# Conv FFN up products: one 512-column matmul for both input parts, bank copies on ScalarE, add and scale on GpSimd

## The reference, cut to what matters

```python
def conv_ffn(h, w_up, conv_w, conv_b, w_down):
    S = h.shape[1]
    u = h @ w_up
    up = jnp.pad(u, ((0, 0), (CONV_WIDTH_2 - 1, 0), (0, 0)))
    uc = conv_b + sum(conv_w[j] * up[:, j:j + S] for j in range(CONV_WIDTH_2))
    gate, val = uc[..., :D_FF_2], uc[..., D_FF_2:]
    return (jax.nn.silu(gate) * val) @ w_down
```

## Time and profile before

| | us |
|---|---|
| median of 3 runs (lowest to highest) | 1089.23 (1089.05 to 1089.32) |
| span of the profiled execution, first to last instruction | 1086.7 |
| PE busy in it | 1078.6 |
| DVE busy in it | 773.8 |
| ACT busy in it | 641.4 |
| POOL busy in it | 21.5 |

### The profile page before, as it was taken

One profiled execution on the slowest core, in us unless ns is written; L12 is line 12 of the kernel. 1 busy time (PEld: TensorE's weight loads), 2 busy tenths in 40 slices (PEclk: granted clock), 3 DMA queues, 4 the chain that ended last, 5 costly groups with the idle time before them and its releaser, 6 DMA issues.

```text
span 1086.7 us, 19341 instructions
## 1 busy us (share of the span) xinstructions
PE 1078.6 (99%) x7124; PEld 944.0 (87%) x7124; DVE 773.8 (71%) x1390; ACT 641.4 (59%) x1105; POOL 21.5 (2%) x47
## 2 busy tenths in 40 slices
PE   9999999999999999999999999999999999999998
PEld 8967899999988887888888999999877789999997
DVE  5977765555567767666756977878876757787876
ACT  5577664444466567566566555555766756555553
POOL 0000000000000000000010000000001000000000
PEclk9999999999999999999999999999999999999999
DMA  9642566666646563365515566565553435656562
GB/s 318 192 132 81 172 195 193 190 182 187 193 118 213 157 210 101 115 191 180 174 60 155 176 194 193 158 209 186 164 193 110 143 117 175 202 167 211 171 196 97
DMA packets 117774, 183.90 MB, mean 169 GB/s; under 512 B 6864, under 2 KB 70736, under 8 KB 117584
## 3 DMA queue, kind: packets, MB, share of 16 engines
q1 hardware_dynamic: 117280, 182.77, 53.7%
q10 hardware_dynamic: 432, 0.29, 0.1%
HBM read 181.99 MB, written 1.05 MB: 168 GB/s over the span
## 4 chain that ended last, share of the span: by engine, by line
PE 90%; DVE 6%; ACT 3%; issue 1%; DMA 1%; SPq 0%; DVEq 0%; ACTq 0%
PE ps L722 11%; PE ps L724 10%; PE ps L723 10%; PE ps L750 9%; PE ps L752 9%; PE ps L751 9%; PE ps L811 5%; PE ps L812 5%; PE ps L813 5%; DVE w_lo L1901 3%; PE ps L913 2%; PE ps L890 1%; PE ps L943 1%; PE ps L986 1%; DVE hid L2421 1%; ACT w_hi L1299 1%
## 5 line engine op out<-in xcount | busy, mean ns | idle before, releaser
L1901 DVE TENSOR_TENSOR w_lo<-w_stage,w_hi 128x1024 fp32r<-128x1024 f32 x336 | 403.5, 1221 | 171.0 <-ACT w_hi L1299 170.0
L1299 ACT ACTIVATE w_hi<-w_stage 128x1024 fp32r<-128x1024 f32 x336 | 349.1, 1054 | 172.0 <-PE ps L724 75.6
L750 PE MATMUL ps<-aT_hi,w_hi 128*128 128x256 f32 x992 | 281.6, 284 | 0.6 <-issue 0.4
L752 PE MATMUL ps<-aT_hi,w_lo 128*128 128x256 f32 x992 | 280.8, 283 | 0.0
L751 PE MATMUL ps<-aT_lo,w_hi 128*128 128x256 f32 x992 | 280.8, 283 | 0.0
L722 PE MATMUL ps<-w_hi,aT_hi 128*128 128x512 f32 x480 | 192.9, 402 | 1.9 <-DVE aT_lo L1915 1.3
L750 PEld LDWEIGHTS ps<-aT_hi,w_hi 128*128 128x128 f32 x992 | 190.3, 192 | 2.3 <-DVE w_lo L1901 0.7
L751 PEld LDWEIGHTS ps<-aT_lo,w_hi 128*128 128x128 f32 x992 | 190.3, 192 | 1.0
L752 PEld LDWEIGHTS ps<-aT_hi,w_lo 128*128 128x128 f32 x992 | 190.3, 192 | 0.0
L724 PE MATMUL ps<-w_hi,aT_lo 128*128 128x512 f32 x480 | 187.5, 391 | 0.0
L723 PE MATMUL ps<-w_lo,aT_hi 128*128 128x512 f32 x480 | 187.1, 390 | 0.0
(11 more groups left out here) (252 smaller groups left out, 1108.0 us busy)
## 6 DMA issues: line engine op xcount, KB each, us to landing
w_stage<-in_ffn_w_up SPq DMA_DIRECT2D x88, 512.0 KB, 4.7
w_stage<-in_a_w_qkv SPq DMA_DIRECT2D x72, 512.0 KB, 4.1
w_stage<-in_ffn_w_down SPq DMA_DIRECT2D x44, 512.0 KB, 3.5
w_stage<-in_w_up SPq DMA_DIRECT2D x32, 512.0 KB, 3.9
w_stage<-in_w_down SPq DMA_DIRECT2D x32, 512.0 KB, 4.3
w_stage<-in_b_w_qkv SPq DMA_DIRECT2D x24, 512.0 KB, 4.1
w_stage<-in_w_in SPq DMA_DIRECT2D x23, 512.0 KB, 5.1
w_stage<-in_w_out SPq DMA_DIRECT2D x8, 512.0 KB, 3.5
```

What stands on the lines that cost most here:

```text
L750: pe.matmul(o, wh, aT_hi[:, k, :], start=(k == 0), stop=False)
L752: last = pe.matmul(o, wl, aT_hi[:, k, :], start=False, stop=(k == KT - 1))
L1299: act.activation(w_hi[:, slot, :], w_in[:, slot, :], ACT.Copy).then_inc(hi_done[slot], 1)
L1901: dve.tensor_tensor(w_lo[:, slot, :], w_in[:, slot, :], w_hi[:, slot, :].bitcast(F32), ALU.subtract).then_inc(lo_done[slot], 1)
```

## The change

In the FFN's head and loop (ten of the eleven groups of each layer) the first two matmuls of a triple become one: `aT_hi` and `aT_lo` now lie side by side in one tensor `aT`, and the high weights meet both in one matmul with 512 moving columns. It writes a whole bank: the left half gets hi x hi (and later lo x hi), the right half hi x lo. The two halves are added afterwards: ACT copies the whole bank to SBUF (`both`, in the space of `xn`) and frees it, POOL adds the halves in place and then multiplies with `rbc` into `scaled`. DVE's `scale_up` goes away in these groups. ACT's `taps` wait for POOL (`scaled`). POOL waits for ACT's copy and for the taps of the group before, which read the same `scaled`; ACT's copy waits until POOL has read the same part of `both` for the group before. The weight splits move somewhat among these steps. The tail group keeps its three matmuls and DVE's `scale_up`.

```diff
-        aT_hi = sb("aT_hi", [P, KT, S], F32R)
-        aT_lo = sb("aT_lo", [P, KT, S], F32R)
+        aT = sb("aT", [P, KT, 2, S], F32R)
+        aT_hi, aT_lo = aT[:, :, 0, :], aT[:, :, 1, :]
...
+        both = xn[:].rearrange("p t (f s) -> p (t f) s", s=2 * S)
...
-                            pe.matmul(o, wh, aT_hi[:, k, :], start=(k == 0), stop=False)
-                            pe.matmul(o, wh, aT_lo[:, k, :], start=False, stop=False)
+                            if fold:
+                                pe.matmul(ps[:, bank(stg, names[f]), :], wh, aT[:, k, :, :].rearrange("p a s -> p (a s)"),
+                                          start=(k == 0), stop=False)
+                            else:
+                                pe.matmul(o, wh, aT_hi[:, k, :], start=(k == 0), stop=False)
+                                pe.matmul(o, wh, aT_lo[:, k, :], start=False, stop=False)
                             last = pe.matmul(o, wl, aT_hi[:, k, :], start=False, stop=(k == KT - 1))
...
-                dense_cols(S_, 0, 4, B4)
+                dense_cols(S_, 0, 4, B4, fold=True)
...
+            def second_half(stg, i, names, f):
+
+                act.wait_ge(*is_full(stg, names[f], i))
+                act.activation(both[:, f, :], ps[:, 4 + f, :], ACT.Copy).then_inc(drained[4 + f], 1)
...
+                def halves(stg, i, names, n, fs):
 
                     for f in fs:
-                        act.wait_ge(*is_drained(stg, names[f], i))
+                        if stg is not st["ffn_a_head"] or n > 1:
+                            act.wait_ge(s["scaled"], at(stg, "scaled", 4 * (n - 2) + f + 1, i))
+                        second_half(stg, i, names, f)
+
+                def taps(stg, i, names, j, n, fs):
+
+                    for f in fs:
+                        if n is None:
+                            act.wait_ge(*is_drained(stg, names[f], i))
+                        else:
+                            act.wait_ge(s["scaled"], at(stg, "scaled", 4 * (n - 1) + f + 1, i))
...
                 def convolve(stg, i, n0, names, j, n):
 
                     split(stg, n0, i)
-                    taps(stg, i, names, j, (0, 1))
+                    halves(stg, i, names, n, (0, 1))
                     split(stg, n0 + 1, i)
+                    taps(stg, i, names, j, n, (0, 1))
                     split(stg, n0 + 2, i)
                     gate(stg, i, n)
-                    taps(stg, i, names, j, (2, 3))
+                    halves(stg, i, names, n, (2, 3))
                     split(stg, n0 + 3, i)
+                    taps(stg, i, names, j, n, (2, 3))
...
+            def scale_up(stg, i, names, n):
+
+                for f in range(4):
+                    pool.wait_ge(*is_drained(stg, names[f], i))
+                    pool.tensor_tensor(both[:, f, 0:S], both[:, f, 0:S], both[:, f, S:2 * S], ALU.add)\
+                        .then_inc(s["half"], 1)
+                    pool.wait_ge(s["conv"], at(stg, "conv", 4 * (n - 2) + f + 1, i))
+                    pool.wait_ge(s["half"], at(stg, "half", 4 * (n - 1) + f + 1, i))
+                    pool.tensor_tensor(scaled[:, f, :], both[:, f, 0:S], rbc[:], ALU.mult).then_inc(s["scaled"], 1)
+
+            def scale_ffn(tag):
+
+                S_ = st[f"ffn_{tag}_head"]
+                pool.wait_ge(*is_drained(st[f"norm_ffn_{tag}"], "scale"))
+                scale_up(S_, 0, A4, 1)
+                scale_up(S_, 0, B4, 2)
+                S_ = st[f"ffn_{tag}_loop"]
+                with trips(pool, S_) as i:
+                    scale_up(S_, i, A4, 1)
+                    scale_up(S_, i, B4, 2)
...
                 def convolve(stg, i, n0, names, j, n):
 
                     split(stg, n0, i)
-                    scale_up(stg, i, names, (0, 1))
                     split(stg, n0 + 1, i)
                     taps(stg, i, j, n, (0, 1))
                     split(stg, n0 + 2, i)
-                    scale_up(stg, i, names, (2, 3))
+                    split(stg, n0 + 3, i)
                     taps(stg, i, j, n, (2, 3))
                     product(stg, i, n)
-                    split(stg, n0 + 3, i)
```

More of the change, by code:

```diff
@@ L287, in ffn @@
         up = {"cv": 4, "conv": 4, "silu": 1, "u": 1, "uhi": 1, "ulo": 1, "dve_step": 4}
+        folded = {**up, "half": 4, "scaled": 4}
         return [
@@ L448, in blocks_kernel @@
             "orstd", "osq", "hms", "dm", "ovar", "sig", "sq", "ms8", "rs8", "silu", "u", "uhi", "ulo", "msq", "pms", "prstd", "x_new",
-            "lam", "zeroed", "const_ready", "gate_w", "unit", "rd", "rdb", "bc", "ohi", "olo")}
+            "half", "scaled", "r2", "lam", "zeroed", "const_ready", "gate_w", "unit", "rd", "rdb", "bc", "ohi", "olo")}
         def is_full(stg, name, i=0):
@@ L732, in dense_rows, with dense_cols @@
                         after[q]()
-            def dense_cols(stg, i, n0, names, turned=None, after=None, order=BY_PAIRS, each=None):
+            def dense_cols(stg, i, n0, names, turned=None, after=None, order=BY_PAIRS, each=None, fold=False):
                 for q, (pair, deep) in enumerate(order):
@@ L1236, in ffn @@
                 with trips(pe, S_) as i:
-                    dense_cols(S_, i, 0, A4)
+                    dense_cols(S_, i, 0, A4, fold=True)
                     await_hidden(S_, 0, i)
                     down(S_, i, 4, range(2))
-                    dense_cols(S_, i, 6, B4)
+                    dense_cols(S_, i, 6, B4, fold=True)
                     await_hidden(S_, 1, i)
@@ L1744, in ffn @@
                 keep_scale(st[f"norm_ffn_{tag}"])
-                taps(S_, 0, A4, 0, (0, 1))
+                halves(S_, 0, A4, 1, (0, 1))
                 split(S_, 2)
+                taps(S_, 0, A4, 0, 1, (0, 1))
+                halves(S_, 0, A4, 1, (2, 3))
+                split(S_, 3)
                 gate(S_, 0, 1)
-                taps(S_, 0, A4, 0, (2, 3))
-                split(S_, 3)
+                taps(S_, 0, A4, 0, 1, (2, 3))
                 hidden_hi(S_, 0, 1, 0, W)
-                splits(S_, range(4, 6))
-                taps(S_, 0, B4, 1, (0, 1))
-                splits(S_, range(6, 8))
+                split(S_, 4)
+                halves(S_, 0, B4, 2, (0, 1))
+                split(S_, 5)
+                taps(S_, 0, B4, 1, 2, (0, 1))
+                split(S_, 6)
                 gate(S_, 0, 2)
-                taps(S_, 0, B4, 1, (2, 3))
+                halves(S_, 0, B4, 2, (2, 3))
+                split(S_, 7)
+                taps(S_, 0, B4, 1, 2, (2, 3))
                 splits(S_, range(8, 10))
@@ L1767, in ffn @@
                 split(S_, 0)
-                taps(S_, 0, A4, U2 - 1, (0, 1))
+                taps(S_, 0, A4, U2 - 1, None, (0, 1))
                 split(S_, 1)
                 gate(S_, 0, 1)
-                taps(S_, 0, A4, U2 - 1, (2, 3))
+                taps(S_, 0, A4, U2 - 1, None, (2, 3))
                 split(S_, 2)
@@ L1882, in wide_parts @@
                     low_part(stg, units, j)
+            A4, B4 = [f"a{f}" for f in range(4)], [f"b{f}" for f in range(4)]
+            def scale_up(stg, i, names, n):
[15 more added lines that the diff above has]
+                    scale_up(S_, i, B4, 2)
             for hf in range(2):
                 wide_parts(st[f"half_a{hf}"], list(units_a(hf)))
+            scale_ffn("a")
             for hf in range(2):
                 wide_parts(st[f"half_b{hf}"], list(units_b(hf)))
+            scale_ffn("b")
         @block.vector
@@ L2464, in ffn @@
                 split(S_, 6)
-                scale_up(S_, 0, B4, (2, 3))
                 split(S_, 7)
```

13 lines of the change are left out of this document (4 added, 9 removed).

## The result

The changed kernel took 1125.36 us (median of 4 runs, 1124.09 to 1125.96), the kernel before 1089.28 us beside it. The ratio is 1.0331, 95% interval 1.0320 to 1.0343. The forecast was 1133 us. The profiled execution has a span of 1122.2 us.

What follows compares the result with a forecast made beforehand. DVE and POOL, sharing one time line, were taken to replace PE as the bound: 15.5 us loop, 3.8 head and 2.7 tail per layer, 44 us for two, added to 1089.2 us gave 1133 us, range 1098 to 1160.

Steps and rivals of the forecast that it cites:

- PE, the fold: FFN triples on PE: 0.360 to 0.347 us each, 13.3 ns less, 8.5 us over 640 triples if PE stays the bound.
- ACT, four copies, "none on the path": FFN loop: four more copies of 0.59 us per group fit ACT's idle time; cost on the path none.
- DVE, 12.4 us left: FFN loop: with four scalings gone, DVE's splits, taps and other work take 12.4 us per group.
- POOL, 0.73 us each: FFN groups: eight more POOL operations at 0.73 us each, 5.84 us per group, which taken alone fits.
- DVE and POOL exclude each other: FFN: DVE operations with two SBUF inputs and POOL's work on SBUF wait for each other, sharing one time line.
- A group of 18.5 us: FFN loop: 12.4 DVE + 5.84 POOL + 0.24 hand-overs make 18.5 us, +1.55 us per group against 16.96.
- Head and tail: Per layer: head +1.6 us for later taps and +2.2 us for DVE's missing idle time; tail +2.7 us.
- The first (no contention): Rival, FFN: no contention worth naming, PE stays the bound, faster at 1084 us (1081 to 1088); chance 0.12.
- The third, "worse": Rival, FFN: taps wait for `scaled`, splits queue behind, DVE and POOL idle together; 1157 up to 1180 us; chance 0.06.
- The clock: Part of the worse rival: PE idling 2 us of 18.5, in pieces, might lower its clock; within chance 0.06.
- The second (it cancels): Rival: POOL holds DVE about 0.5 us, head and tail eat the fold's gain; 1089 us; chance 0.04.
- the fourth (no saving of the fold): Rival, PE: the 512-column matmul takes 2 x 0.120 us; first rival then gives 1092 us; inside the other chances.

Runs made afterwards that it cites:

- complete version on DVE: Kernel before plus the fold, GpSimd unused: ACT copies the right half, DVE adds the left half from PSUM and multiplies; 1083.81 us, ratio 0.9951.
- single-column variant: Changed kernel with each GpSimd operation replaced by a single-column addition, all waits kept, sum of halves and scaling left out; 1084.15 us, ratio 0.9956.
- the copies early: Changed kernel with ACT's bank copies of the value half moved ahead of the weight split and SiLU in the loop; 1106.54 us, ratio 1.0165.
- additions beside the kernel before: Kernel before with eight 128x256 GpSimd additions per group set beside it, results unused and no other engine waiting; 1121.82 us, ratio 1.0301.
- little of the exclusion: Changed kernel with each GpSimd operation replaced by a one-column addition and a 620-column memset, waits kept, sum and scaling left out; 1110.16 us, ratio 1.0192.
- two kernels that fold without GpSimd: Kernel before with only the fold, right half left out: 1086.16 us; with the complete computation on ACT and DVE: 1083.81 us.
- kernel with the early heads: Changed kernel with early loop copies, plus split 4 and group B's first copies ahead of rounding group A's product in the heads; 1103.84 us.

## Why the prediction was right, and where it was not

- **PE, the fold.** Mis-sized: 13.3 ns per triple were taken, 6.5 or 13 measured, mostly 6.5, and 2.8 us (5.3 in the complete version on DVE) in the place of 8.5. In the forecast this term was lost in the waits, so it did not enter the sum.
- **ACT, four copies, "none on the path".** This step failed. The idle time took in the busy time, as said, but not the place in the queue: the copies stand behind a rounding and a SiLU that wait for DVE, and GpSimd waits for the copies. Moving two of them saves 18.8 us.
- **DVE, 12.4 us left.** In the single-column variant DVE is busy 11.9 to 12.2 of 17 us. Right.
- **POOL, 0.73 us each.** Right where nothing disturbs it (730 ns), though the earlier trace rows show 0.74 and 0.87. Up to 1.7 us otherwise. The pause before a multiplication, taken as 0.05 us, is 0.14 to 0.15 at 704.03 and 712.39 us.
- **DVE and POOL exclude each other.** Right in the main, and both ways, as forecast: the DVE side in the taps' 648 ns, the GpSimd side in the addition of 1.72 us at 713.23, which outlasts the split that began at 713.04 by its own 0.6 us.
- **A group of 18.5 us.** Measured 18.1 to 18.3, but by another mechanism. Between 699.87 and 718.15, gaps in which neither works sum to 2.06 us, so their time line is not full. The forecast added up busy times; what acts is the ring, and that its length with blocked legs is close to the sum is luck. The sum is also longer than what the pair needs: with the copies early, the same operations of DVE and GpSimd, 12.4 + 5.84 = 18.2 us by the forecast, pass in groups of 17.0 us, and DVE or GpSimd is busy in 16.1 of them (695.39 to 712.45 us). So their records overlap by some 2 us per group, and an operation does not shut the other out for its whole length; which part of it runs during the wait was not measured. Where the time line does fill (the additions beside the kernel before), the pace is nearly the same.
- **Head and tail.** Head: 3.8 plus 2 x 1.55 makes 6.9 us, measured 7.1 and 7.2; but the forecast's reasons were the later first taps and DVE's lack of idle time, and 6.6 of it is there with little of the exclusion and gone with a short leg. So the leg is the reason, which the first of the two names in part, and that the size fits is luck. Loop: 8 x 1.55 = 12.4, measured 12.2 and 11.2. Tail: +2.7 was taken, and 1.7 us came back. PE does wait 2.45 us there, as forecast, but it came there less late than DVE: its last matmul of the loop's down quarters starts at 785.61 us (before 770.73), 14.9 us late, where the product is 17.6 late. So the wait closes that difference and is no further loss. These 4.4 us per layer are the difference between 22.0 and 17.6, and with it most of that between 1133 and 1125.
- **The rivals.** The first (no contention) is refuted by the additions beside the kernel. The third, "worse", named the mechanism (taps wait for `scaled`, splits stand behind, both idle) and gave it 0.06 as an addition to the sum; it stands in its place. The clock, which that rival named too, falls in the profile for one short stretch (last section). The second (it cancels) is refuted by the time itself, the fourth (no saving of the fold) by the two kernels that fold without GpSimd.

## What to carry to other kernels

Add up busy times to see whether an engine has room, but then follow one group from its product to the next through every queue: a step that waits for another engine counts with its whole length once the ring that it closes is longer than the work of the busiest engine, however idle its own engine is. Before work goes to GpSimd, look at which DVE instructions read SBUF twice; here the addition belonged on DVE, with one operand from PSUM. If a helper engine must be in the chain, put the instructions that feed it ahead of those that wait for its consumer.

## What the runs showed of the hardware that was not expected

Matmuls of 512 columns between 256-column ones run in two paces, 0.3535 or 0.347 us per triple at granted clock 1.00, and a pace lasts until the stream is broken. What chooses it stays open; no run was made for it.

At the tail of layer b, PE idles 2.47 us for `u_lo`, and then its granted clock falls. The busy time by stretch (us; busy and instructions of PE, PEld, DVE, ACT, POOL; clock; DMA) and PE's timeline:

```profile
1109.00:1112.00 3.00, 0.53 (x3) 0.36 (x3) 2.97 (x5) 2.15 (x3) 0.00 (x0) 0.98 0.00 0
1112.00:1116.00 4.00, 4.00 (x12) 2.94 (x11) 1.37 (x2) 0.71 (x1) 0.00 (x0) 0.58 0.01 3
```

```profile
1111.59 0.55 PE L798 MATMUL ps<-w_hi,u_hi 128*128 128x512 f32 x1 [2.47 <-DVE u_lo L2540]
1111.94 0.63 PE L799 MATMUL ps<-w_lo,u_hi 128*128 128x512 f32 x1
1112.37 0.63 PE L800 MATMUL ps<-w_hi,u_lo 128*128 128x512 f32 x1
```

The matmuls stand 0.43 us apart, not 0.227: that is the level of 1.2 GHz, for some 3.5 us, and costs about 1.6 us (eight matmuls, 0.2 us each). The same wait of 2.45 us in layer a, at 788.45 us, is followed by clock 1.00. In the kernel with the early heads both waits of 2.5 us at the tails are followed by a granted clock of 0.50 (at 777.5 and at 1091.5 us). What decides it stays open. The profiled execution took 1124.09 us at a mean clock of 0.998; the three others took 1.2 to 1.9 us more at 0.994 or 0.995, so they seem to hold more such stretches.
